# Router logits with stationary weights in four column groups, fewer filler products, three steps moved to ScalarE, one weight tile loaded ahead of the gather

## The reference, cut to what matters

```python
def expert_choice_moe(h, w_router, w_gate, w_up, w_down):
    cap = CAPACITY_FACTOR * T // N_EXPERTS                      # 128
    logits = jnp.einsum('btd,de->bte', h, w_router)             # (1024 tokens, 16 experts)
    affinity = jax.nn.softmax(logits, axis=-1)
    gate, idx = lax.top_k(jnp.swapaxes(affinity, 1, 2), cap)
    xe = jax.vmap(lambda hb, ib: hb[ib])(h, idx)                # gather 128 rows for each expert
    a = jnp.einsum('becd,edf->becf', xe, w_gate)
    u = jnp.einsum('becd,edf->becf', xe, w_up)
    ye = jnp.einsum('becf,efd->becd', jax.nn.silu(a) * u, w_down) * gate[..., None]
    return scatter_add(ye, idx)
```

## Time and profile before

| | before |
|---|---|
| time, median of 3 runs | 2776.96 us (2775.77 to 2777.18) |
| the profiled execution | 2776.52 us |
| its span | 2774.8 us |
| PE busy | 2724.0 us, 98% |
| DVE / ACT / POOL busy | 1993.5 / 1302.2 / 544.3 us |
| chain that ended last | PE 86%, DVE 7% |
| DMA from 2227 to 2700 us | 395 to 403 GB/s |

### The profile page before, as it was taken

The page is one execution under the profiler, slowest core; times in us unless marked ns, Lnnn a source line. Parts: engine busy times, 40 slices in busy tenths (PEclk is TensorE's granted clock), DMA queues, the critical chain, the costliest instruction groups (busy, mean ns, idle before and its releaser), DMA issues.

```text
span 2774.8 us, 35402 instructions
## 1 busy us (share of the span) xinstructions
PE 2724.0 (98%) x13776; PEld 2196.1 (79%) x13776; DVE 1993.5 (72%) x2823; ACT 1302.2 (47%) x2029; POOL 544.3 (20%) x507
## 2 busy tenths in 40 slices
PE   8999999999999999999999999999999899999998
PEld 7777778787778888988888887777788678888886
DVE  5344455888776688878867756665666789999997
ACT  5444533433323455443222246555423467777775
POOL 0011111745455110511011111000100410000000
PEclk9999999999999999999999999999999999999999
DMA  5111113345661998233222253101664699999997
GB/s 169 37 47 31 46 66 124 107 138 152 180 187 58 347 301 238 90 107 103 95 76 69 76 189 93 47 31 54 193 233 152 233 403 397 397 396 397 396 397 271
DMA packets 270634, 494.12 MB, mean 178 GB/s; under 512 B 30140, under 2 KB 141908, under 8 KB 269956
## 3 DMA queue, kind: packets, MB, share of 16 engines
q1 hardware_dynamic: 240864, 396.40, 41.0%
q0 software_dynamic: 29456, 95.43, 10.6%
q10 hardware_dynamic: 148, 0.04, 0.0%
HBM read 424.60 MB, written 67.21 MB: 177 GB/s over the span
## 4 chain that ended last, share of the span: by engine, by line
PE 86%; DVE 7%; issue 2%; ACT 2%; POOL 2%; DMA 1%; POOLq 0%; DVEq 0%; SPq 0%; ACTq 0%
PE PS L133 80%; PE PS L136 6%; DVE m L142 4%; POOL m L142 2%; ACT m L139 2%; DVE m L148 1%; DMA m<-in_w_down_dram 0%; DMA m<-in_w_mod_dram 0%; DVE m L181 0%; DVE m L157 0%; DVE m L151 0%; DVE m L145 0%; ACT L139 0%; DMA m<-in_w_exp_up_dram 0%; DMA m<-in_x_dram 0%
## 5 line engine op out<-in xcount | busy, mean ns | idle before, releaser
L133 PE MATMUL PS<-m,m 128*128 128x512 f32 (+6 forms) x11722 | 2519.8, 387 | 11.7 <-DVE m L142 3.9
L133 PEld LDWEIGHTS PS<-m,m 128*128 128x128 f32 (+2 forms) x11722 | 1975.9, 184 | 465.7 <-issue 75.2
L139 ACT ACTIVATE m<-m 128x512 fp32r<-128x512 f32 (+5 forms) x886 | 796.7, 920 | 885.5 <-PE PS L133 385.7
L142 DVE TENSOR_TENSOR m<-m,m 128x512 fp32r<-128x512 f32 (+5 forms) x912 | 986.2, 1113 | 214.5 <-ACT m L139 196.2
L139 ACT ACTIVATE m<-PS 128x512 f32<-128x512 f32 (+3 forms) x487 | 276.4, 593 | 397.8 <-PE PS L133 188.0
L142 DVE TENSOR_TENSOR m<-PS,m 128x512 f32<-128x512 f32 (+1 forms) x454 | 299.9, 685 | 182.3 <-PE PS L133 125.5
L142 POOL TENSOR_TENSOR m<-m,m 128x512 f32<-128x512 f32 (+4 forms) x178 | 278.2, 1568 | 608.0 <-DVE m L142 273.5
L136 PE MATMUL PS<-ident,m 128*128 128x128 f32 x1722 | 244.7, 277 | 25.6 <-DVE m L157 8.9
L136 PEld LDWEIGHTS PS<-ident,m 128*128 128x128 f32 x1722 | 200.6, 141 | 78.3 <-issue 27.8
L139 ACT ACTIVATE m<-m,small 128x640 f32<-128x640 f32 (+4 forms) x201 | 156.9, 785 | 117.1 <-DVE small L151 116.6
L157 DVE COPY m<-PS 128x512 f32<-128x512 f32 (+2 forms) x148 | 95.3, 647 | 145.4 <-PE PS L136 119.7
(11 more groups left out here) (106 smaller groups left out, 548.2 us busy)
## 6 DMA issues: line engine op xcount, KB each, us to landing
m<-in_w_exp_gate_dram SPq DMA_DIRECT2D x64, 1024.0 KB, 9.1
m<-in_w_exp_up_dram SPq DMA_DIRECT2D x64, 1024.0 KB, 9.1
m<-in_w_exp_down_dram SPq DMA_DIRECT2D x64, 1024.0 KB, 9.5
m<-in_w_mod_dram SPq DMA_DIRECT2D x48, 512.0 KB, 3.8
m<-in_w_gate_up_dram SPq DMA_DIRECT2D x44, 512.0 KB, 5.9
m<-in_w_in_dram SPq DMA_DIRECT2D x21, 1024.0 KB, 5.3
m<-in_w_in_dram SPq DMA_DIRECT2D x25, 512.0 KB, 5.2
x_scratch<-m POOLq DMA_DIRECT2D x24, 512.0 KB, 4.2
```

The costliest lines, as they stand in the source:

```text
L133: return Unsent() if self.e is None else self.e.matmul(o, l, r, start=first, stop=last, **k)
L139: return Unsent() if self.e is None else self.e.activation(o, i, fn, **k)
L142: return Unsent() if self.e is None else self.e.tensor_tensor(o, a, b, op)
```

## The change

The logits are computed with the weights stationary. For each k the 16 weight columns of k and those of a neighbouring k (32 columns) are loaded into column group k % 4 of PE's array, and the 128 columns of `x3T` move; the four partial sums lie in PSUM partitions 0 to 127 (32 for each group), of which 16 in each group count. ACT copies this 128x128 result to `lgT` (`lt_out`; DVE for tile 7, `lt_taken`), and a new step `("pick", i)` multiplies it with a 0/1 matrix `picked`, which adds the four parts and transposes them back to `lg_acc` of 128x16. `ROUTE` is written anew with `pick` and with `row`, `rank`, `tally` and `choose` at other places. For tile 7 the multiplication and the column copy of the softmax are on ACT. `top_idf` and `top_taken` are on ACT (`top_number`, `top_copied`). The fillers are 3 and 14 instead of 14 and 18. Tile 4 of the weights is loaded and split by ACT ahead of the gather. `jrev` is made later, on POOL ahead of the gather. In the first expert `find8` of round 15 stands between the two `hidden`.

```diff
+        def wr_pair(k):
+            k0 = k - (k % 4 == 3)
+            return wr2[:, k0:k0 + 2, :].rearrange("p a n -> p (a n)")
...
                 elif what == "route":
...
                     for k in range(k0, k1):
-                        t = pe.matmul(ps("lg_acc", i)[:, 0:16], x3T[i % 2][:, k, :], wr2[:, k, :], k == 0, k == 7)
+                        part4 = slice(32 * (k % 4), 32 * (k % 4) + 32)
+                        t = pe.matmul(ps("lt_acc", i)[part4, 0:128], wr_pair(k), x3T[i % 2][:, k, :], k < 4, k > 3,
+                                      skip_group_check=True)
                     if k1 == 8:
-                        t.then_inc(*pe.did("lg_acc", i))
+                        t.then_inc(*pe.did("lt_acc", i))
+                elif what == "pick":
+                    bank_of["lg_acc", i] = pe.bank("lg_raw", i)
+                    pe.wait_ge("masks", "picked")
+                    pe.wait_ge(*partial_taken(i))
+                    pe.matmul(ps("lg_acc", i)[:, 0:16], lgT, picked, True, True).then_inc(*pe.did("lg_acc", i))
...
+                elif what == "route" and part[1] == 8 and i < 7:
+                    act.wait_ge("lt_acc", i)
+                    if i:
+                        act.wait_ge("lg_acc", i - 1)
+                    act.activation(lgT, ps("lt_acc", i)[:, 0:128], ACT.Copy).then_inc(*act.did("lt_out", i))
                 elif what == "choose":
                     act.wait_ge("lg_shifted", i)
                     act.activation(aff_of(i), aff_of(i), ACT.Exp, accum_out=e3[:, i:i + 1]).then_inc(*act.did("lg_exp", i))
+                    if i == 7:
+                        act.wait_ge("softmax_scale")
+                        act.wait_ge("row_turned", 6)
+                        act.activation(column, first_column(7).to_broadcast([128, 128]), ACT.Copy, scale=e3[:, 7:8]).then_inc(
+                            *act.did("last_column"))
+                        act.wait_ge("last_column")
+                        act.activation(aff_of(7), aff_of(7), ACT.Copy, scale=e3[:, 7:8]).then_inc(*act.did("last_softmax"))
...
-                 ("out", 7, 1, 0, 4), ("tally", 5), ("route", 6, 0, 8), ("turn", 7, 0), ("choose", 6), ("out", 7, 1, 4, 8),
+                 ("out", 7, 1, 0, 4), ("route", 6, 0, 8), ("turn", 7, 0), ("row", 5), ("rank", 5), ("out", 7, 1, 4, 5),
+                 ("pick", 6), ("choose", 6), ("out", 7, 1, 5, 8), ("tally", 5), ("row", 6), ("pair", 1), ("pair", 2),
...
             if n < 2:
                 sp.wait_ge("w_low", W_END - 2 + n)
-            elif n < 4:
+            elif n < 5:
                 sp.wait_ge("o2p_acc", 7, 1)
...
         def router_pe(pe):
-            keep_busy(pe, 14)
+            keep_busy(pe, 3)
...
-            keep_busy(pe, 18)
+            keep_busy(pe, 14)
...
         def router_act(act):
+            e_high(act, 4)
             turn_x_act(act, 0)
-            for n in range(4, 8):
+            for n in range(5, 8):
...
             hidden(dve, 0, 0)
+            find8(dve, 15)
             hidden(dve, 0, 1)
-            find8(dve, 15)
-            dve.wait_ge("top_found", 15)
-            dve.tensor_copy(idf[0:32], idx[0:32].bitcast(U32)).then_inc(*dve.did("top_idf"))
-            dve.wait_ge("top_turned")
-            dve.tensor_copy(vT, ps("top_turned")[:, 0:64]).then_inc(*dve.did("top_taken"))
...
                 elif what == "turn_h":
-                    for k0 in (0, 4):
-                        hb_round(act, e, k0)
+                    if e == 0:
+                        act.wait_ge("top_found", 15)
+                        act.activation(idf[0:32], idx[0:32].bitcast(U32), ACT.Copy).then_inc(*act.did("top_number"))
+                    hb_round(act, e, 0)
+                    if e == 0:
+                        act.wait_ge("top_turned")
+                        act.activation(vT, ps("top_turned")[:, 0:64], ACT.Copy).then_inc(*act.did("top_copied"))
+                    hb_round(act, e, 4)
```

More of the change, by code:

```diff
@@ L3485, in program @@
                  ("out", 1, 1, 0, 8), ("turn", 0, 0), ("turn", 0, 4), ("norm", 1),
[L3486 to L3494, removed]
@@ L3495, in program @@
-                 ("out", 7, 0, 0, 8), ("turn", 6, 0), ("turn", 6, 4), ("pair", 1), ("row", 5), ("rank", 5),
-                 ("out", 7, 1, 0, 4), ("tally", 5), ("route", 6, 0, 8), ("turn", 7, 0), ("choose", 6), ("out", 7, 1, 4, 8),
-                 ("row", 6), ("pair", 2), ("route", 7, 0, 4), ("turn", 7, 4), ("norm", 7), ("rank", 6), ("route", 7, 4, 8),
-                 ("choose", 7), ("tally", 6), ("row", 7), ("pair", 3), ("rank", 7), ("tally", 7)]
+                 ("out", 2, 1, 0, 8), ("route", 0, 0, 8), ("turn", 1, 0), ("turn", 1, 4), ("norm", 2),
@@ new lines, in program @@
+                 ("out", 3, 0, 0, 8), ("pick", 0), ("choose", 0), ("route", 1, 0, 8), ("turn", 2, 0), ("turn", 2, 4),
+                 ("out", 3, 1, 0, 8), ("row", 0), ("rank", 0), ("pick", 1), ("choose", 1), ("route", 2, 0, 8), ("norm", 3),
+                 ("out", 4, 0, 0, 8), ("row", 1), ("rank", 1), ("pick", 2), ("choose", 2), ("turn", 3, 0), ("turn", 3, 4),
+                 ("out", 4, 1, 0, 8), ("tally", 1), ("row", 2), ("rank", 2), ("route", 3, 0, 8), ("norm", 4),
+                 ("out", 5, 0, 0, 8), ("tally", 2), ("pick", 3), ("choose", 3), ("turn", 4, 0), ("turn", 4, 4),
@@ new lines, in program @@
+                 ("out", 5, 1, 0, 8), ("row", 3), ("rank", 3), ("route", 4, 0, 8), ("norm", 5),
+                 ("out", 6, 0, 0, 8), ("tally", 3), ("pick", 4), ("choose", 4), ("turn", 5, 0), ("turn", 5, 4),
+                 ("out", 6, 1, 0, 8), ("row", 4), ("rank", 4), ("route", 5, 0, 8), ("norm", 6), ("pair", 0),
+                 ("out", 7, 0, 0, 8), ("pick", 5), ("turn", 6, 0), ("turn", 6, 4), ("choose", 5), ("tally", 4),
+                 ("out", 7, 1, 0, 4), ("route", 6, 0, 8), ("turn", 7, 0), ("row", 5), ("rank", 5), ("out", 7, 1, 4, 5),
@@ L3501, in program @@
+                 ("pick", 6), ("choose", 6), ("out", 7, 1, 5, 8), ("tally", 5), ("row", 6), ("pair", 1), ("pair", 2),
+                 ("route", 7, 0, 4), ("turn", 7, 4), ("norm", 7), ("rank", 6), ("route", 7, 4, 8), ("pick", 7), ("choose", 7),
+                 ("tally", 6), ("row", 7), ("pair", 3), ("rank", 7), ("tally", 7)]
         R_BANK = 0
@@ L3716, in out2_dve @@
                     if i >= 2:
-                        dve.wait_ge("lg_acc", i - 2)
+                        dve.wait_ge("lt_acc", i - 2)
                     dve.tensor_copy(x3T[i % 2][:, 0:4, :], turned("x3_turned", i, 0)).then_inc(*dve.did("x3T_out_v", i, 0))
+                elif what == "pick" and i == 7:
+                    dve.wait_ge("lt_acc", 7)
+                    dve.wait_ge("lg_acc", 6)
+                    dve.tensor_copy(lgT, ps("lt_acc", 7)[:, 0:128]).then_inc(*dve.did("lt_taken"))
                 elif what == "choose":
@@ L3729, in out2_dve @@
                     dve.wait_ge("lg_exp", i)
[L3730 removed]
+                    dve.reciprocal(e, e).then_inc(*dve.did("softmax_scale" if i == 7 else "dve_order~"))
+                    if i == 7:
+                        continue
                     dve.wait_ge("dve_order~")
```

64 lines of the change are left out of this document (41 added, 23 removed).

## The result

The changed kernel takes **2762.24 us** (median of 5 runs, 2761.76 to 2764.19), the kernel before 2777.1. The ratio is 0.9946, with a 95% interval of 0.9934 to 0.9959: faster by 0.54%. One run of the kernel before, at 3424 us, is left out of the ratio. The profiled execution took 2762.24 us with a span of 2760.5; before it was 2776.52 and 2774.8.

What follows compares the result with a forecast made beforehand. PE was taken as the bound in `out2` and the experts, with waits on DVE, POOL and fillers between; terms -4.0 + 1.0 + 0.9 - 2.75 - 2.85 - 5.1 - 0.5 + 0.5 = -12.8 us gave 2764, range 2757 to 2771.

Steps and rivals of the forecast that it cites:

- Route: In `out2`: route with pick 1.26 us instead of 1.79, seven times; with `tally` and `pair` moved, -4.0 us together.
- four groups to be no better than two: Assumption for `out2`'s route: records keep the two-group pitch of 0.060 us, giving 1.04 us a route; lower bound 0.62.
- four groups overlap fully: Rival for `out2`'s routes: four column groups run at half the pitch, 2.9 us more gain, 2761; chance 0.14.
- The order on DVE: End of `out2`: `rank` 5 and `choose` 6 now stand ahead of the last `x3_gated`; +1.0 us (0 to +1.6).
- `choose` 7: Seam after `out2`: extra copy and pick push its subtraction behind POOL's start, where it stalls; +0.9 us (-0.6 to +1.2).
- Fillers: Seam before the first expert: 3 fillers instead of 14 let `rank_out` end sooner; -2.75 us (-1.9 to -3.6).
- Tile 4: First expert: tile 4 ahead in POOL's chain removes both waits in `up`, ending 24.9 us behind the first product; -2.85 us.
- Cast and copies: First expert, `up` to `down`: on ACT they avoid the wait for POOL, 2.9 us instead of 8.0; -5.1 us.
- The gather of expert 1 is late next: Expert 1's gather, queued behind POOL's chain, lands 13.2 us behind `up`; PE waits 1 to 2.5 us.
- the clock of `down`: First expert: full clock shortens `down`'s 36 records from 11.06 to 8.3 us, but the late gather leaves only -0.5 us.
- The end: Kernel's end: last scatter meets a queue still full of weights, so final loads come up to 1 us later; +0.5 us.
- the rival that the stream binds: Experts: gain beyond the weight stream's 7.5 us earlier start is lost if PE reaches its reserve; 2769.5, chance 0.14.

Runs made afterwards that it cites:

- experiment 1: Changed kernel with the route's products in two column groups instead of four; 2766.86 us.
- experiment 7: Changed kernel with the old 14 and 18 fillers instead of 3 and 14; 2765.75 us.
- experiment 6: Changed kernel with weight tile 4 loaded and split behind the gathered rows again; 2767.19 us.
- experiment 5: Changed kernel with the cast of the found numbers back on DVE, the copy still on ACT; 2763.81 us.
- experiment 9: Changed kernel with the load of weight tile 12 held until `up` of expert 0 has its first half out; 2775.33 us.
- experiment 10: Changed kernel with the load of weight tile 12 held until `down` of expert 0 is at tile 9; 2780.05 us.
- experiments 9 to 12: Changed kernel: two with weight tile 12's load held (2775.33, 2780.05 us), one with expert 1's gather sooner (2764.19), one with that plus 4 fillers (2762.34).
- experiment 8: Changed kernel with 5 fillers behind the last half route and 8 behind the pick and `tally` 6; 2761.23 us.

## Why the prediction was right, and where it was off

The forecast was 2764 and the time 2762.24: the predicted chain of causes held but for one wait (the gather's, below), the sum was 1.5 us short (-12.8 against -14.3). Part of that closeness is luck: 3.1 us of gains taken too low or costs too high, most of it in the route, stand against 1.7 us of gains taken too high. Step by step:

- **Route: the mis-sized term.** The step "four groups to be no better than two" is wrong. Four groups gave 0.57 us, just under the lower bound (0.62) of the text, and the last `out` ended 6.4 us sooner, not 4.0. The argument (two records of a product need the same group) costs nothing, since records of the other groups run meanwhile; the 0.060 of the earlier trace rows is the pitch of two groups (1.00 / 16 in experiment 1), and I read it as a limit of the array. The rival "four groups overlap fully" described this mechanism and gave 2761. The Trainium skill, TensorEngine Tiling (Array Packing), section Theoretical Speedup, has up to 4x for 32 columns; the runs show 1.85 / 0.57 = 3.2x, the rest being, by the fit, the 0.15 us that doesn't shrink.
- **The order on DVE:** +0.54 (g stands 0.74 behind the last `out`, not 0.20), predicted +1.0. **`choose` 7:** +0.71, predicted +0.9, by the predicted stall. Neither the new order nor the move of tile 7's softmax to ACT was undone alone; these shares are read from distances.
- **Fillers:** `rank` 7's start to the end of `rank_out` -1.97, predicted -2.75 with -1.9 as its bound. `rank_out` ran at the lower clock throughout and took 3.41 us; the range went to 3.5, the value had 2.7. Undoing the fillers cost 2.9 us (experiment 7), as the old 14 would also run at the lower clock now.
- **Tile 4:** F to the end of `up` 24.82 us, predicted 24.9; worth 4.5 and not 2.85 when undone alone (experiment 6), as it brings the gather forward too.
- **Cast and copies:** `up` to `down` 3.63 us instead of 8.0, -4.4, predicted -5.1. The cause, a cast held by POOL, is shown by experiment 5.
- **The gather of expert 1 is late next:** the wait of 2.13 us is in the 1 to 2.5 foretold, and T1 was almost indifferent to the clock of `down`, as foretold: over the traces that keep tile 4 and the cast as changed, its 36 records take 8.45 to 11.33 us and F to T1 stays within 38.11 and 39.74. But the text had the gather behind POOL's chain, issued 4.8 us behind `up` and landing at 13.2. The chain did allow 4.8 (4.61 + 0.16); the list, which the text took as ready, allowed 5.4, and the landing took 8.8 us and not 8.4. So T1 is 14.2 us behind `up`, not 13.3, and that is the 0.9 us by which cast and clock together fell short.
- **The end:** +0.45, predicted +0.5. But of the rival that the stream binds, the text said "the reserve should be over 10 us". For a PE wait on tiles a pause of 7 us bears that out (experiment 9); in experiment 10, with 16 us, PE did wait. For the final loads there was no such reserve: experiments 9 to 12 show that hardly anything was left. The rival didn't decide only because the change ends where the floor begins.
- Fillers and cast were taken 1.5 us too well and the clock 0.2, order and `choose` 0.65 too badly: +1.0 left, beside the route's -2.4; 0.1 is left over in small steps.

Left open are why the clock falls behind the filled seam in experiment 8 and whether the stream's start can be brought ahead of the gathered rows without delaying them. No run here bears on either.

## What to carry to other kernels

For products with few output columns, count column groups: here the time divided nearly by the number of groups, even though each product is two records. Neighbouring products in program order were always in different groups; another order was not tried. When work is taken off VectorE or moved in time beside POOL, ask which VectorE operation meets POOL's interval next; here moving the cast to ScalarE removed the stall, and moving POOL in time only handed it on. When an instruction waits for two things, take the distance to each over several variants: the one that stays constant is what it waits for (the gather stood 1.17 us behind the list, and with a chain that ended 5 us sooner it moved only as far as the list did). And when a transfer queue is full over the whole stage, compare the distance from its start to the end over several variants: where it no longer changes, the queue's start is the next thing to try.

## What the runs showed of the hardware beyond expectation

- Four column groups: 16 records of 128 moving columns in 0.57 us, 0.036 each, though each record still lasts 279 ns from start to end (278 in two groups).
- A VectorE operation of 128x1 on SBUF operands stood 1.62 and 1.74 us for POOL. In the same stretches a reciprocal of 128x1 kept its 0.16 us, and so did the max and index searches of 32x512 (0.67 us) beside POOL's chain of 22.75 us.
- 14 fillers (28 records), nearly all at the lower clock, took 6.20 us in experiment 7 and 4.84 in the changed kernel with the rise of the clock in their midst, against 36 records of 4.26 at the full clock. `rank_out` behind 3 fillers at the lower level takes 3.41 us.
- With the DMAs at the same share (1.03), a tile's landing went from 9.1 to 14.6 and up to 21 us while PE waited for no tile (2300 to 2700 us); the price showed first in the small transfers at the end, a scatter of 8.4 to 9.1 us instead of 6.3.
